# A hybrid RWKV-7 / conformer encoder layer with a mixture of experts: the order of VectorE's work in an expert block, the place of the shared expert's down products, and the order of routing

## The reference, cut to what matters

```python
x = layer_norm(alpha * x + (1.0 + gt1) * mix, ln1_w, ln1_b)
u2 = layer_norm(x) * (1.0 + sc2) + sh2
# moe_ffn
scores = sigmoid(ut @ router_w);  sel = scores + router_b          # 512 x 64
grp_score = sum of the two best of each group of 8 experts         # 8 groups
emask = experts of the 4 best groups
eidx = top 8 experts of sel within emask
w_sel = scores[eidx] / sum(scores[eidx]) * 2.5
routed = sum over the 8 experts e of w_sel[e] * (silu(u @ gate[e]) * (u @ up[e])) @ down[e]
shared = (silu(ut @ sh_gate) * (ut @ sh_up)) @ sh_down
x = layer_norm(alpha * x + (1.0 + gt2) * (routed + shared), ln2_w, ln2_b)
```

## Time and profile before

| | us |
|---|---|
| median of 3 runs | 2193.1 (2193.03 to 2198.47) |
| the profiled execution, device time | 2198.09 |
| its span, first to last instruction | 2196.1 |
| TensorE busy | 1933.9 (88% of the span) |
| VectorE busy | 1427.4 (65%) |
| ScalarE busy | 880.6 (40%) |
| GpSimd busy | 676.7 (31%) |
| mean granted clock of TensorE | 0.954 of full speed |

### The profile page before, as it was taken

How to read it: one execution, slowest core, us unless ns; L and a number is a source line. 1 busy time by engine, 2 the same in 40 slices (tenths; PEclk the granted TensorE clock), 3 DMA queues, 4 the chain that set the end, 5 groups by cost and what they waited for, 6 DMA issues and landing times. The chain is left out here.

```text
span 2196.1 us, 54472 instructions
## 1 busy us (share of the span) xinstructions
PE 1933.9 (88%) x20438; PEld 1427.2 (65%) x20438; DVE 1427.4 (65%) x2794; ACT 880.6 (40%) x1468; POOL 676.7 (31%) x534
## 2 busy tenths in 40 slices
PE   5699999968499999999997777999999999999955
PEld 1576777736399899889983535666666666666622
DVE  2689888943255665656544637777777777777718
ACT  0322333132345554454430015555555555555500
POOL 4544445301443435343401201221222222212214
PEclk9899999989699999999998788999999999999977
DMA  5644554214100011000006018888889888888845
GB/s 196 196 140 143 175 182 138 75 53 139 58 21 21 4 31 31 21 26 19 14 13 225 39 53 348 328 332 331 317 331 327 316 310 323 311 317 317 310 184 240
DMA packets 163089, 382.08 MB, mean 174 GB/s; under 512 B 23700, under 2 KB 97602, under 8 KB 135537
## 3 DMA queue, kind: packets, MB, share of 16 engines
q1 hardware_dynamic: 141444, 341.70, 43.1%
q0 software_dynamic: 21152, 37.80, 4.9%
q10 hardware_dynamic: 335, 0.22, 0.0%
HBM read 363.09 MB, written 55.34 MB: 191 GB/s over the span
## 5 line engine op out<-in xcount | busy, mean ns | idle before, releaser
L2002 DVE TENSOR_TENSOR moe_w_lo<-moe_raw,moe_w_hi 128x1024 fp32r<-128x1024 f32 x272 | 315.0, 1220 | 4.0 <-ACT moe_w_hi L1919 2.5
L1919 ACT ACTIVATE moe_w_hi<-moe_raw 128x1024 fp32r<-128x1024 f32 x272 | 265.3, 1047 | 59.9 <-DMA moe_raw<-in_exp_up 57.8
L1863 PE MATMUL moe_pH<-moe_w_hi,moe_x_hi 128*128 128x512 f32 x544 | 220.9, 406 | 45.8 <-DVE moe_x_lo L2009 36.1
L1797 POOL DMA_INDIRECT moe_xg<-scratch_u2d,moe_idx x70 | 70.9, 1013 | 585.5 <-DVE moe_y L2019 562.9
L621 DVE SCALAR_TENSOR_TENSOR proj_hc<-proj_hp,cwT,proj_hc 128x256 f32 x480 | 245.9, 586 | 7.9 <-DVE proj_st L594 7.9
L1873 PE MATMUL moe_pY<-moe_wd,moe_hT 128*128 128x512 f32 x544 | 246.3, 596 | 0.5 <-ACT moe_hT L1934 0.5
L419 POOL TENSOR_TENSOR proj_w_lo<-proj_w,proj_w_hi 128x1024 fp32r<-128x1024 f32 x59 | 175.4, 2977 | 215.3 <-ACT proj_w_hi L503 215.3
L446 PE MATMUL proj_bank<-proj_u_hi,proj_w_hi 128*128 128x512 f32 x536 | 212.4, 396 | 25.8 <-DVE proj_u_lo L652 12.2
L1863 PE MATMUL moe_pH<-moe_w_lo,moe_x_hi 128*128 128x512 f32 x544 | 213.6, 393 | 0.0
L1863 PE MATMUL moe_pH<-moe_w_hi,moe_x_lo 128*128 128x512 f32 x544 | 213.6, 393 | 0.0
L446 PE MATMUL proj_bank<-proj_u_hi,proj_w_lo 128*128 128x512 f32 x536 | 210.5, 393 | 0.0
(11 more groups left out here) (336 smaller groups left out, 3699.6 us busy)
## 6 DMA issues: line engine op xcount, KB each, us to landing
moe_raw<-in_exp_gate SPq DMA_DIRECT2D x69, 1024.0 KB
moe_raw<-in_exp_up SPq DMA_DIRECT2D x69, 1024.0 KB, 9.5
moe_wd<-in_exp_down SPq DMA_DIRECT2D x68, 1024.0 KB
proj_w<-in_w_in SPq DMA_DIRECT2D x59, 512.0 KB, 5.3
proj_aw<-in_ada_w SPq DMA_DIRECT2D x8, 2048.0 KB
last_yb<-scratch_ybuf SPq DMA_DIRECT2D x4, 2560.0 KB, 23.3
mod_aw<-in_ada_w SPq DMA_DIRECT2D x4, 2048.0 KB, 18.9
scratch_rkv<-proj_st SPq DMA_DIRECT2D x24, 256.0 KB, 2.2
```

Source lines behind the costliest of these rows:

```text
L1797: pool.indirect_dma_start(out=xg[q][:], out_offset=None, in_=g["u2d"][:], in_offset=bass.IndirectOffsetOnAxis(ap=idx[q][:, 0:1], axis=0), ...
L1863: ins = nc.tensor.matmul(pH[:], a[:, k], w[p][:, k].rearrange("p w f -> p (w f)"), start=(k == 0 and n == 0), stop=(k == KC - 1 and n == 2))
L1919: nc.scalar.activation(w_hi[p][:, ks].rearrange("p k w f -> p w k f"), raw[p][:, :, ks], ACT.Copy) \
L2002: nc.vector.tensor_tensor(w_lo[p][:, ks].rearrange("p k w f -> p w k f"), raw[p][:, :, ks], w_hi[p][:, ks].rearrange("p k w f -> p w k f") ...
```

## The change

It has three parts. In the expert stage `place_y` moves on VectorE behind `rows` and `read_y`, to the end of a block, and the wait for its own result moves to the next `read_y`. The shared expert's down products move from the routing stage to the start of the last stage's TensorE list, where they open the sums in PSUM; `hT` and the down weights lie in `u1T` until then, and the scratch tensor `acc` with its stores and loads is gone. In the routing stage VectorE routes the four tiles without the products between them, and TensorE does the gate and up products of the second half between the small routing matmuls. In the last stage the transfers of 3 rows come ahead of those of 5, ScalarE applies the norm (a scale and a shift) in place of VectorE, and VectorE adds the pair of rows of the last tile itself.

```diff
 # mix_and_route, SP
-            for t in range(TT):
-                sp.wait_ge(y_read, 2 * t + 2)
-                sp.dma_start(g["acc"][t * P:(t + 1) * P], yo[:, t]).then_inc(y_out, 16)
+            sp.wait_ge(mixed, TT)
+            sp.dma_start(g["shd"], sh_down[0].rearrange("(c p) n -> p c n", p=P)).then_inc(shd_in, 16)
...
 # mix_and_route, TensorE
+            for w in range(2):
+                shared_up(0, w)
             pe.wait_ge(consts, 4 + SLOTS)
             pe.wait_ge(a_ready, TT)
+            for t in range(TT):
+                ins = nc.tensor.matmul(bank[2][0:E, 0:1], A[:, t], ones[:, 0:1], start=(t == 0), stop=(t == TT - 1))
+            ins.then_inc(cnt_done, 1)
             for t in range(TT):
                 o = bank[3][:, t * E:(t + 1) * E]
...
+            shared_up(1, 0)
             pe.wait_ge(nb_ready, 1)
-            nc.tensor.matmul(bank[4][0:E, 0:1], upto[0:E, 0:E], nb[:], start=True, stop=True).then_inc(ci_done, 1)
+            nc.tensor.matmul(bank[0][0:E, 0:1], upto[0:E, 0:E], nb[:], start=True, stop=True).then_inc(ci_done, 1)
+            shared_up(1, 1)
             pe.wait_ge(m_ready, 1)
...
 # mix_and_route, VectorE
-                if t < 2:
-                    v.wait_ge(h_done, 2 * t + 2)
-                    v.wait_ge(sh_silu, t + 1)
-                    nc.vector.tensor_tensor(hT[:, t], hs[:, t], bank[5 + 2 * t][:], ALU.mult).then_inc(up_read, 1)
...
+            def shared_product(f):
+                v.wait_ge(h_done, 2 * f + 2)
+                v.wait_ge(sh_silu, f + 1)
+                nc.vector.tensor_tensor(hT[:, f], hs[:, f], bank[5 + 2 * f][:], ALU.mult).then_inc(up_read, 1)
+
+            v.wait_ge(mixed, TT)
+            shared_product(0)
             v.wait_ge(cnt_done, 1)
...
 # moe, VectorE
                 nc.vector.tensor_copy(gcol[q][:], val[:, bass.ds(b, 1), 2]).then_inc(y_ready, 1)
-                ch.wait()
-                v.wait_ge(y_ready, b + 1)
...
             def read_y(b, q, n):
                 v.wait_ge(y_free[q], n + 1)
                 v.wait_ge(d_done, 2 * b + 2)
+                v.wait_ge(y_ready, b + 1)
                 nc.vector.tensor_scalar(y[q][:, 512:D], pY[1][:], gcol[q][:, 0:1], None, ALU.mult).then_inc(y1_read, 1)
...
                 x_low(b + 1)
-                place_y(b, p, i)
                 rows(b + 3, 1 - p)
                 read_y(b - 1, 1 - p, i + (p - 1))
+                place_y(b, p, i)
...
 # last_norm, SP
             for t in range(TT):
+                sp.dma_start(yb[:, t, ON_PE:], y3[t * P:(t + 1) * P, ON_PE:]).then_inc(yb_in[2 * t + 1], 16)
                 sp.dma_start(yb[:, t, 0:ON_PE], y3[t * P:(t + 1) * P, 0:ON_PE]).then_inc(yb_in[2 * t], 16)
-                sp.dma_start(acc[:, t], g["acc"][t * P:(t + 1) * P]).then_inc(acc_in[t], 16)
-                sp.dma_start(yb[:, t, ON_PE:], y3[t * P:(t + 1) * P, ON_PE:]).then_inc(yb_in[2 * t + 1], 16)
...
 # last_norm, TensorE
             for t in range(TT):
+                for h in range(2):
+                    for f in range(2):
+                        nc.tensor.matmul(bank[2 * t + h][:], g["u1T"][:, f, t * P:(t + 1) * P],
+                                         g["shd"][:, f, h * 512:(h + 1) * 512], start=(f == 0), stop=False)
...
 # last_norm, ScalarE
+                act.wait_ge(ready, t + 1)
+                nc.scalar.activation(acc[:, t], acc[:, t], ACT.Identity, scale=rstd[:, t:t + 1], bias=shift[:, t:t + 1]) \
+                  .then_inc(normed, 1)
...
 # last_norm, VectorE
-                v.wait_ge(acc_in[t], 16)
                 v.wait_ge(yb_in[2 * t + 1], 16)
-                v.wait_ge(paired, t + 1)
-                for k in (TOP_K - 1, ON_PE):
-                    ch(nc.vector.tensor_tensor(acc[:, t], acc[:, t], yb[:, t, k], ALU.add))
+                if t < TT - 1:
+                    v.wait_ge(paired, t + 1)
+                else:
+                    ch(nc.vector.tensor_tensor(yb[:, t, ON_PE], yb[:, t, ON_PE], yb[:, t, ON_PE + 1], ALU.add))
+                ch(nc.vector.tensor_tensor(acc[:, t], yb[:, t, ON_PE], yb[:, t, TOP_K - 1], ALU.add))
...
-                nc.vector.tensor_scalar(acc[:, t], acc[:, t], mv[:, t, 0:1], rstd[:, t:t + 1], ALU.subtract, ALU.mult) \
-                  .then_inc(normed, 1)
+                nc.vector.scalar_tensor_tensor(shift[:, t:t + 1], mv[:, t, 0:1], -1.0, rstd[:, t:t + 1], ALU.mult, ALU.mult) \
+                  .then_inc(ready, 1)
```

More of the change, by code:

```diff
@@ L1557, in _, with shared_up @@
                 ins.then_inc(logit, 1)
[L1559 to L1575, removed]
+            pe.wait_ge(sh_in, 32)
+            def shared_up(f, w):
+                for k in range(KC):
+                    ins = nc.tensor.matmul(bank[4 + 2 * f + w][:], shw[:, k, w, f * P:(f + 1) * P], u2T[:, k],
+                                           start=(k == 0), stop=(k == KC - 1))
+                ins.then_inc(h_done, 1)
+            for w in range(2):
+                shared_up(0, w)
             pe.wait_ge(consts, 4 + SLOTS)
             pe.wait_ge(a_ready, TT)
+            for t in range(TT):
+                ins = nc.tensor.matmul(bank[2][0:E, 0:1], A[:, t], ones[:, 0:1], start=(t == 0), stop=(t == TT - 1))
+            ins.then_inc(cnt_done, 1)
             for t in range(TT):
@@ L1672, in _ @@
                 ch.mark(nc.vector.tensor_tensor_scan(rk[:, t], ones[:, 0:E], A[:, t], 0.0, ALU.mult, ALU.add))
-                if t < 2:
-                    v.wait_ge(h_done, 2 * t + 2)
-                    v.wait_ge(sh_silu, t + 1)
-                    nc.vector.tensor_tensor(hT[:, t], hs[:, t], bank[5 + 2 * t][:], ALU.mult).then_inc(up_read, 1)
-            for t in range(TT):
-                v.wait_ge(pos_done, TT)
-                nc.vector.scalar_tensor_tensor(g["pos"][:, :, t], bank[3][:, t * E:(t + 1) * E], 1.0, A[:, t],
-                                               ALU.add, ALU.mult).then_inc(pos_read, 1)
+            def shared_product(f):
[4 more added lines that the diff above has]
+            shared_product(0)
             v.wait_ge(cnt_done, 1)
@@ L1686, in _ @@
             v.sem_inc(nb_ready, 1)
+            for t in range(TT):
+                v.wait_ge(pos_done, TT)
+                nc.vector.scalar_tensor_tensor(g["pos"][:, :, t], bank[3][:, t * E:(t + 1) * E], 1.0, A[:, t],
+                                               ALU.add, ALU.mult).then_inc(pos_read, 1)
             def own(c):
@@ L2054, in last @@
                 product(b)
+                read_y(b - 1, 0, i)
                 place_y(b, 1, i)
-                read_y(b - 1, 0, i)
                 read_y(b, 1, i)
@@ L2068, in last_norm @@
         rows = g["last_rows"]
+        yb = s.sb("yb", [P, TT, TOP_K, D])
         acc = s.sb("acc", [P, TT, D])
-        yb = s.sb("yb", [P, TT, TOP_K, D])
         st = s.sb("st", [P, TT, 2, 6])
         mv = s.sb("mv", [P, TT, 2])
-        rstd = s.sb("rstd", [P, TT])
+        rstd, shift = s.sb("rstd", [P, TT]), s.sb("shift", [P, TT])
         bank = [s.ps(f"bank{i}") for i in range(8)]
-        normed, scaled, last_ready, var_done, std_done, out_ready, stored, dve, summed, paired = (s.sem(n) for n in (
-            "normed scaled last_ready var_done std_done out_ready stored dve summed paired").split())
-        acc_in = [s.sem(f"acc_in{t}") for t in range(TT)]
+        (normed, scaled, last_ready, var_done, std_done, ready, out_ready, stored, dve, summed, paired) = (s.sem(n) for n in (
+            "normed scaled last_ready var_done std_done ready out_ready stored dve summed paired").split())
         yb_in = [s.sem(f"yb_in{n}") for n in range(2 * TT)]
@@ L2102, in _ @@
                         ins = nc.tensor.matmul(bank[2 * t + h][:], g["ident"][:], yb[:, t, k, h * 512:(h + 1) * 512],
[L2103 removed]
+                                               start=False, stop=(k == ON_PE - 1))
                     ins.then_inc(summed, 1)
@@ L2143, in _, with shift_rows @@
         def _(pool):
-            def shift(t):
+            def shift_rows(t):
                 pool.wait_ge(normed, t + 1)
@@ L2148, in shift @@
                 nc.gpsimd.tensor_tensor(acc[:, t], acc[:, t], rows[:, 2], ALU.add).then_inc(out_ready, 1)
-            for t in range(TT):
+            for t in range(TT - 1):
                 pool.wait_ge(yb_in[2 * t + 1], 16)
                 nc.gpsimd.tensor_tensor(yb[:, t, ON_PE], yb[:, t, ON_PE], yb[:, t, ON_PE + 1], ALU.add).then_inc(paired, 1)
-                if t >= 2:
-                    shift(t - 2)
-            shift(TT - 2)
+                if t >= 1:
+                    shift_rows(t - 1)
+            shift_rows(TT - 2)
 _INS = """x c ada_w ada_b w_in shift_mu w0 w_up a0 a_up g_up k_k k_a r_k lnx_w lnx_b conv_w conv_b cnorm_w
```

37 lines of the change are left out of this document (14 added, 23 removed).

## The result

The changed kernel takes 2164.11 us (median of 4 runs, 2161.84 to 2166.63) against 2193.07 before: the ratio is 0.9843, with a 95% interval of 0.9821 to 0.9865. It is 29 us faster, where 85 were forecast, and lies above the range of 2095 to 2141. The profiled execution has a span of 2164.2 us, 31.9 less than before.

A forecast was written before the change was run, and what follows sets the result against it. The prediction took TensorE to bound most of an expert-stage interval, with waits for VectorE, late behind scatter landings, as the rest. Routing 20, expert stage 58 and last stage 7 summed to 85 us, giving 2108, range 2095 to 2141.

The forecast's parts named there:

- Routing: Routing stage: reordered products and routing tiles finish the table's last write 20 us earlier, bounds 18 and 21.
- The expert stage: Expert stage: moving `place_y` shortens a block from 11.33 to 10.45 us, 58 us over 66 intervals; at best 71.
- So TensorE's 10.25 becomes the pace: Expert stage: TensorE's own 10.25 us a block sets the interval, at best 71 us gained; 10.45 taken for DMA load.
- the landing + 1.31 + about 0.3: Expert stage, GpSimd holding its gather until the scatter landed: 9.5 us a block at the median, 10.5 at landing 8.91.
- rival 3: Expert stage: GpSimd's hold for the landed scatter makes the kernel slower if landings average above 10.1 us; chance 0.03.
- The weights' chain: Expert stage: `raw` lands 9.5 us after issue, reaching ScalarE 1.8 us into a block, with 1.5 us before `x_lo`.
- Rival 2: Expert stage: the wait at `place_y` only moves and the stage gives nothing; 27 us in all, 2166; chance 0.07.
- Rival 1: Expert stage: DMA becomes the pace, ScalarE waiting for `raw`; 10.9 us a block, stage gives 28, 2138; chance 0.20.
- Rival 4: Last stage: the 32 product records run at 1.2 GHz, taking 28 us, and it loses 3 to 5; 2119; chance 0.08.
- The last stage: Last stage: `acc` transfers gone, down products in TensorE's idle time, shorter tail on VectorE: 7 us, bounds 9 and -5.
- at about 2174.5: Last stage: time in us when VectorE, doing its first two adds beside a working GpSimd, reaches the last tile's sums.

The follow-up runs named there:

- The kernel with the scatter first: Changed kernel with GpSimd issuing the scatter ahead of the gather and waiting for its landing after both; ratio 0.9702 to the kernel before.
- the kernel with raw ahead: Changed kernel with SP loading block b+2's gate and up weights ahead of its wait for the down products; ratio 0.9708 to the kernel before.
- the two single edits: Changed kernel with either scatter ahead of gather on GpSimd, or gate and up loads issued earlier on SP; ratios 0.9702 and 0.9708 to the kernel before.
- both edits: Changed kernel with scatter ahead of gather on GpSimd and gate and up loads issued earlier on SP; 2101.04 us, ratio 0.9571 to the kernel before.
- The kernel without GpSimd's two operations: Changed kernel without the product with ln2's weight and the sum with its bias for the last stage's first three tiles; one execution, 2158.8 us.
- second run: The changed kernel itself, unaltered, measured again on the chip of two other experiments; ratio 0.9837 to the kernel before.

## Why the prediction was wrong

*Routing: right.* 20 us forecast, 20.8 measured, by the steps named: four tiles of VectorE in 16.3 us beside the first half, counting behind it at 1272.5, the table 18.5 us later. The waits for the masks and for the semaphores were within 1 us.

*The expert stage: wrong, and here the forecast failed.* 58 us forecast, 8.5 measured. The failing step is "So TensorE's 10.25 becomes the pace", and the term under it that was mis-sized is GpSimd's own list, "the landing + 1.31 + about 0.3, 9.5 us at the median". It measured 8.46 + 1.36 + 1.43 = 11.25 us, above TensorE's 10.25, and it set the pace in every block. No row stood behind the 0.3: from a scatter's landing to GpSimd's next transfer it takes 1.43 us, and that alone makes the list 10.7 us at the landing of before. The other part is the landing, which grew from 7.87 to 8.46 us, where I had held it fixed; so the move's 0.65 us came back nearly whole. I had named this loop in rival 3, as a danger only above a landing of 10.1, because of the 0.3. The kernel with the scatter first shows the loop as the cause: with only the gather and its hold taken out from between, the interval falls to 10.66.

The weights' chain was mis-sized too, but it is not what failed. I had `raw` landing 9.5 us after its issue, 1.8 us into a block, with 1.5 us to spare. Its median became 10.0 and ScalarE's longest wait 3.5 us, beyond the reserve. Yet in the kernel after none of TensorE's waits leads back to it. Its issue counts there by way of the scatter's landing, as the kernel with raw ahead shows, and its lateness reaches TensorE only once the scatter goes first. Hence the two single edits give 31 and 30 us and the pair 60: one shortens the loop around the landing, the other the landing, and only both bring the loop below 10.25.

*The rivals.* Rival 2, "the wait only moves", at 2166, is what the time looks like (2164), and it had 0.07. That its number came so near is luck: it adds 20, 0 and 7 us, and measured were 20.8, 8.5 and 2.3. Its mechanism was right in part: the wait shrank by a quarter, and scatters that landed later took most of the gain back. Rival 1 had ScalarE's wait for `raw` right (it nearly doubled) and the reason wrong: the engines were not full. The version with both edits moves 353 GB/s against 327 after, with a share of 0.91 against 0.89 where I had taken 0.96 for a wall. Rival 3 had the right place and one size wrong, as said above. Rival 4 did not come: the 32 records of products took 16.57 us in the last stage, against 17.4 forecast.

*The last stage: right in its mechanism, wrong in size.* Forecast 7 us, measured 2.3. TensorE's sums of the last tile were ready 52.0 us after the first transfer's issue (51.6 forecast). The mis-sized term is VectorE's. The prediction has it at the last tile's sums "at about 2174.5", 53.2 us after the first transfer's issue; it was there after 56.3 (at 2147.99). The product and the residual of tiles 1 and 2 took it 2.3 to 3.4 us each beside GpSimd, and the prediction names no term for that. From the sums to its end it took 12.6 us, not 10.6, as the last tile's product and residual took 5.2 us and not 3.2. The kernel without GpSimd's two operations came to the sums after 50.3 us. On this the Trainium skill ("SBUF — State Buffer", section "SBUF: two separate sides") says that a VectorE operation with two SBUF inputs and a GpSimd operation that reads SBUF exclude each other on a shared port pair for the whole instruction, rather than sharing it. The trace agrees: VectorE's row of 3.25 us at 2151.28, for what alone takes 1.23, ends 1.09 us after GpSimd's of 3.20 us at 2150.24.

## What to carry to other kernels

Where an engine's list holds for a landed transfer, measure the whole loop through that engine, with the time from the landing to its next issue taken from a row, and ask what else can stand between issue and hold: here swapping the scatter and the gather gave 31 us and moving the waiting instruction 8 us. To find out whether such a loop is the pace, look at the time from each landing to the next issue: if it is the same in every block, the engine waits for nothing else. Take the landing's mean for the sum, not its median, and do not hold it fixed: it moved by 0.5 to 1 us with the order and the bytes of other transfers. A wait that grows on another engine is no proof of a second chain; follow the bound engine's own waits back. A step that a profile shows to be 14.0 us long is worth only what did not run beside it: here 4 to 7.

## What the runs showed of the hardware

The indirect scatter of 128 rows of 4 KB, issued by GpSimd, takes 6.5 us to land (median) even with seven eighths of the gate and up loads gone, and 7.9 to 9.2 us beside them; it was longest, 9.2, with the scatter first and `raw` where it was, and 8.2 with both edits. Fewer bytes of down weights sped up the direct loads (10.0 to 8.2 us at the median) and took the late landings from the scatter (longest 11.8 to 9.6 us, mean 8.46 to 7.87), while its median hardly moved. From the landing to the next indirect transfer in GpSimd's list at least 1.2 us passed in every kernel.

TensorE's clock differs from run to run for one and the same list. The 64 records of the router's logits took 13.59 us in the kernel after, at a mean granted clock of 0.51, 11.71 in its second run, and 7.36 at a clock of 1.00 in seven of the experiments, whose lists are the same up to there. The first shared product, right behind them, started anywhere from 1247.7 to 1257.1 us in the kernels with this list. Differences of a few us between two single traces are therefore read inside a stage, and not from its end.
